# First token tiles combined with one-hot products of the last two expert tiles, in a two-layer attention and MoE step on one NeuronCore

## What is computed

```python
for l in range(2):
    x = x + gate_a * attention_l(modulate(rms_norm(x)))
    h = modulate(rms_norm(x))
    # top-1 group of 4, then top-2 experts in it, weights w0, w1
    y = w0 * expert[e0](h) + w1 * expert[e1](h)
    #   expert[e](h) = (silu(h @ w_gate[e]) * (h @ w_up[e])) @ w_down[e]
    x = x + gate_m * y
out = rms_norm(x)
```

## Time and profile before

| What | Value |
|---|---|
| Median of three runs | 1315.37 us (1311.35 to 1317.37) |
| The profiled execution, its own time | 1312.94 us |
| Its span | 1311.1 us |
| PE busy | 1223.5 us, 93% |
| DVE busy | 588.3 us, 45% |
| ACT busy | 412.6 us, 31% |
| POOL busy | 55.9 us |
| Mean DMA rate | 221 GB/s |

### The profile page before, as it was taken

How to read it: one execution, slowest core, us unless ns; L and a number is a source line. 1 busy time by engine, 2 the same in 40 slices (tenths; PEclk the granted TensorE clock), 3 DMA queues, 4 the chain that set the end, 5 groups by cost and what they waited for, 6 DMA issues and landing times.

```text
span 1311.1 us, 17016 instructions
## 1 busy us (share of the span) xinstructions
PE 1223.5 (93%) x5449; PEld 670.6 (51%) x5450; DVE 588.3 (45%) x1352; ACT 412.6 (31%) x847; POOL 55.9 (4%) x63
## 2 busy tenths in 40 slices
PE   5899999999999999998967999799999999999995
PEld 2555566666664475443323444466654574444442
DVE  0431455555543674222317443888835653222216
ACT  2333344444451120111123324677732111111113
POOL 0103000000000020000020000000000110000002
PEclk8999999999999999999987999899999999999997
DMA  9969999622253066999975000500020269989956
GB/s 374 406 261 414 414 412 411 263 98 97 98 216 130 33 251 202 353 352 355 374 303 229 9 0 21 240 1 1 1 97 1 111 227 323 345 286 322 355 225 240
DMA packets 88356, 290.17 MB, mean 221 GB/s; under 512 B 9209, under 2 KB 27580, under 8 KB 86876
## 3 DMA queue, kind: packets, MB, share of 16 engines
q1 hardware_dynamic: 46032, 185.68, 38.5%
q0 software_dynamic: 16640, 64.59, 12.5%
q10 hardware_dynamic: 25612, 38.96, 8.7%
HBM read 214.48 MB, written 74.73 MB: 221 GB/s over the span
## 4 chain that ended last, share of the span: by engine, by line
PE 82%; DMA 5%; DVE 4%; ACT 3%; SPq 2%; issue 2%; POOL 0%; ACTq 0%; DVEq 0%; POOLq 0%
PE ps L2044 16%; PE ps L1668 12%; PE ps L1685 10%; PE ps L2073 8%; PE ps L1621 7%; PE ps L1928 6%; PE ps L1891 4%; PE ps L1713 3%; PE ps L1990 3%; PE ps L1762 3%; PE ps L2125 3%; PE ps L1636 2%; SPq L479 2%; DMA arena<-in_moe_gu 2%; PE ps L1884 2%
## 5 line engine op out<-in xcount | busy, mean ns | idle before, releaser
L2044 PE MATMUL ps<-arena 128*128 (+1 forms) x560 | 246.2, 592 | 0.0
L1621 PE MATMUL ps<-const,arena 128*128 128x128 f32 (+2 forms) x1000 | 145.9, 280 | 38.6 <-DVE arena L1090 17.1
L1621 PEld LDWEIGHTS ps<-const,arena 128*128 128x128 f32 (+2 forms) x1000 | 116.8, 143 | 98.0 <-issue 43.8
L2044 PEld LDWEIGHTS ps<-arena 128*128 128x128 f32 x560 | 103.8, 190 | 117.2 <-issue 117.2
L1668 PE MATMUL ps<-arena 128*128 128x512 f32 (+2 forms) x400 | 155.7, 546 | 8.4 <-DVE arena L1101 4.8
L1139 DVE TENSOR_REDUCE hst<-ps 128x1 f32<-128x640 f32 (+1 forms) x160 | 110.9, 714 | 94.3 <-PE ps L1928 80.2
L1685 PE MATMUL ps<-arena 128*128 128x512 f32 x320 | 142.0, 596 | 1.4 <-issue 1.4
L2073 PE MATMUL ps<-arena 128*128 (+1 forms) x280 | 126.1, 593 | 2.2 <-ACT arena L836 2.2
L723 ACT ACTIVATE arena<-ps,hst 128x640 f32<-128x640 f32 (+1 forms) x160 | 112.4, 706 | 44.0 <-DVE hst L1139 44.0
L1668 PEld LDWEIGHTS ps<-arena 128*128 128x128 f32 x400 | 76.0, 194 | 81.2 <-issue 63.2
L1685 PEld LDWEIGHTS ps<-arena 128*128 128x128 f32 x320 | 59.1, 190 | 69.8 <-issue 69.7
(11 more groups left out here) (211 smaller groups left out, 1187.4 us busy)
## 6 DMA issues: line engine op xcount, KB each, us to landing
arena<-in_moe_gu SPq DMA_DIRECT2D x128, 512.0 KB, 12.6
arena<-in_ada_w SPq DMA_DIRECT2D x62, 768.0 KB, 11.7
slot_rows<-arena POOLq DMA_DIRECT2D x10, 4096.0 KB, 68.4
arena<-in_moe_w_down SPq DMA_DIRECT2D x64, 512.0 KB, 15.4
slot_rows<-arena ACTq DMA_DIRECT2D x33, 512.0 KB, 9.2
arena<-slot_rows ACTq DMA_DIRECT2D x124, 128.0 KB, 13.1
arena<-mod_rows SPq DMA_DIRECT2D x12, 512.0 KB, 10.4
arena<-in_gqa_w_qkv SPq DMA_DIRECT2D x12, 512.0 KB, 14.6
```

What stands on the lines that cost most here:

```text
L1621: return nc.tensor.transpose(out, in_, ident[0:rows, 0:rows])
L2044: last = mm(bank(gu_bank(u)), e_xsT[:, nth(u, D)][:, k * P:(k + 1) * P], w(k * BANK, BANK), start=k == 0, stop=k == KD - 1)
```

## The change

In each layer the first `EARLY[l]` token tiles (one in layer 0, two in layer 1) are combined in two parts. The expert rows that lie in the last two expert tiles (k = 2 and k = 3) aren't gathered. They are taken from `e_y` in SBUF by matmuls with one-hot matrices that hold the tokens' weights. The other rows are gathered already when the store of tile k = 1 has landed. Where a token's row lies in the last two tiles, the gather's index and its weight are made zero.

- `early_tables(l)`, on DVE behind `hid` of k = 1, computes the indices `early_i`, the weights `early_w` and the one-hot matrices `early_hot`.
- PE transposes these matrices in the tail at k = 1 (`early_turned`), DVE copies them to `early_rows`.
- POOL issues `2 * EARLY[l]` gathers once k = 1 is stored, and the rest when the last stores have landed.
- `early_sum` (DVE) weights, gates and adds the gathered part to `xt(t)`; after the last `down` PE multiplies the one-hot matrices with the two last results; `rest_sum` (DVE) gates this part and adds it.
- In layer 1 tiles 0 and 1 leave `last_sums`: their sum stands in `xt(t)`.
- `qkv1` and `qkv2` wait for the last stores, no longer for a gather. `turn_tables` (four DVE instructions, L1261 before) moves behind `mod_cols(1, 0)`.
- Some semaphores of the two layers are merged, with counts to match.

```diff
+EARLY = (1, 2)
...
             if b == 1:
-                sp.wait_ge(gathered(0, 1), gathers(0, 0))
+                sp.wait_ge(S("last_stored"), LAST_STORED)
...
-            pool.wait_ge(S("last_stored"), 16 * (RING_N + 1) * (l + 1))
-            for t in range(NTILE):
+            pool.wait_ge(S("early_tables"), 2 * l + 1)
+            pool.wait_ge(S("prior_stored"), l + 1)
+            pool.wait_ge(S("third_stored"), 16 * (l + 1))
+            for t in range(EARLY[l]):
+                for c in range(2):
+                    pool.indirect_dma_start(
+                        early_e[t][:, c * D:(c + 1) * D], None, slots,
+                        bass.IndirectOffsetOnAxis(ap=early_i[:, 2 * t + c:2 * t + c + 1], axis=0))\
+                        .then_inc(S(f"early_landed{t}"), 16)
+            pool.wait_ge(S("last_stored"), LAST_STORED * (l + 1))
+            for t in range(EARLY[l], NTILE):
...
                 hidT(R * RING_N + k, k)
+                if k == 1:
+                    dve.wait_ge(S("early_turned"), l + 1)
+                    nc.vector.tensor_copy(early_rows[:, 0:2 * EARLY[l] * P], bank(5, 2 * EARLY[l] * P)).then_inc(S("early_ready"), 1)
                 if k + 2 < SLOT_TILES - LOOPED:
                     xsT(R * RING_N + (k + 2), k + 2, R)
                 if k + 1 < SLOT_TILES - LOOPED:
                     hid(R * RING_N + (k + 1), k + 1)
+                if k == 0:
+                    early_tables(l)
...
+            op(nc.vector.tensor_tensor(split(sel, 2), bmid(index, 2), blast(last, TT), ALU.is_equal))
+            op(nc.vector.tensor_tensor(split(sel, 2), split(sel, 2), bmid(s_row, 2), ALU.mult))
+            op(nc.vector.tensor_reduce(rows, split(sel, 2), AX.X, ALU.add))
+            op(nc.vector.tensor_tensor(split(d, 2), bmid(slot, 2), blast(rows, e), ALU.subtract))
...
+            for t in range(n):
+                for i in range(2):
+                    out = hot(early_hot, t, i)
+                    a, b = e * i + 2 * t, e * i + 2 * t + 1
+                    nc.vector.tensor_scalar(out, iota, d[:, a:a + 1], w[:, 2 * t:2 * t + 1], ALU.is_equal, ALU.mult)
+                    op(nc.vector.tensor_scalar(second, iota, d[:, b:b + 1], w[:, 2 * t + 1:2 * t + 2], ALU.is_equal, ALU.mult))
+                    last_hot = op(nc.vector.tensor_tensor(out, out, second, ALU.add))
...
+        def early_sum(l, t):
...
+            nc.vector.tensor_scalar(a, a, early_w[:, 2 * t:2 * t + 1], None, ALU.mult)
+            settle()
+            nc.vector.scalar_tensor_tensor(a, b, early_w[:, 2 * t + 1:2 * t + 2], a, ALU.mult, ALU.add)
+            settle()
+            nc.vector.tensor_tensor(a, a, gate_m[:, v * D:(v + 1) * D], ALU.mult)
+            settle()
+            nc.vector.tensor_tensor(xt(t), xt(t), a, ALU.add)
...
+        def rest_sum(l, t):
...
+                nc.vector.tensor_tensor(rest, rest, gate_m[:, v * D:(v + 1) * D][:, c], ALU.mult)
+                settle()
+                last = nc.vector.tensor_tensor(xt(t)[:, c], xt(t)[:, c], rest, ALU.add)
...
         experts(0)
-        turn_tables()
-        combine(0, 0)
+        early_sum(0, 0)
+        rest_sum(0, 0)
         row_stats("mix1", 0, 1)
+        dve.wait_ge(S("last_stored"), LAST_STORED)
         norm(1, 0)
         mod_cols(1, 0)
+        turn_tables()
         combine(0, 1)
...
-        combine(1, 0)
-        combine(1, 1)
-        for t in range(NTILE):
-            if t + 2 < NTILE:
-                combine(1, t + 2)
-            final(t)
+        for t in range(EARLY[1]):
+            early_sum(1, t)
+        for t in range(EARLY[1]):
+            rest_sum(1, t)
+        final(0)
+        final(1)
+        combine(1, 2)
+        combine(1, 3)
+        final(2)
+        combine(1, 4)
+        final(3)
+        final(4)
...
                 turn_hid(R * RING_N + k, u)
+                if k == 1:
+                    pe.wait_ge(S("early_tables"), 2 * l + 2)
+                    for j in range(2 * EARLY[l]):
+                        last = turn(bank(5, P, j * P), early_hot[:, j * P:(j + 1) * P])
+                    last.then_inc(S("early_turned"), 1)
                 if more:
                     plan_of = gate_up(R * RING_N + (k + 1), u + 1, w, R * RING_N + k)
                 planned_down(R * RING_N + k, u, plan_of, not more)
+
+            pe.wait_ge(S("early_ready"), l + 1)
+            last_t = R * RING_N + (SLOT_TILES - LOOPED - 1)
+            for t in range(EARLY[l]):
+                for n in range(2):
+                    c = slice(n * BANK, (n + 1) * BANK)
+                    mm(bank(sum_bank(t) + n), hot(early_rows, t, 0), last_y[0][:, c], start=True, stop=False)
+                    if t == 0:
+                        pe.wait_ge(S("y_out", l), last_t + (2 + n))
+                    mm(bank(sum_bank(t) + n), hot(early_rows, t, 1), last_y[1][:, c], start=False, stop=True)\
+                        .then_inc(S("rest_made"), 1)
```

More of the change, by code:

```diff
@@ L295, in program, with hot, later @@
     w_pair = e_r[:, R_W:R_W + 2 * NTILE]
-    def gathered(t, c):
-        return S("gathered_first" if t == c == 0 else f"gathered{t}")
+    early_e = (e_xs[:, D:3 * D], e_xsT[:, D:3 * D])
+    early_hot, early_rows, early_tmp = ar(10752, 4 * P), ar(11264, 4 * P), ar(8448, 256)
+    early_w = early_tmp[:, 0:4]
+    last_y = (e_y[:, 2 * D:3 * D], e_y[:, 0:D])
+    LAST_STORED = 16 * 3
+    def hot(rows, t, i):
+        return rows[:, (2 * t + i) * P:(2 * t + i + 1) * P]
+    def later(l, t):
+        return sum(NTILE - n for n in EARLY[0:l]) + t - EARLY[l] + 1
     def gathers(l, t):
-        return (32 if t else 16) * (l + 1)
+        return 32 * sum(t >= n for n in EARLY[0:l + 1])
     def sum_bank(t):
@@ L1564, in experts, with early_tables, new @@
                     hid(R * RING_N + (k + 1), k + 1)
-        def combine(l, t):
+                if k == 0:
+                    early_tables(l)
+        def early_tables(l):
+            n, TT = EARLY[l], SLOT_TILES
+            e = 2 * n
+            stage = ar(14848 + 2 * TT * NE, 4 * TT + NE + 1)
+            s_row, s_rounds = stage[:, 0:TT], stage[:, 4 * TT + NE:]
+            at = [4]
+            def new(cols):
+                at[0] += cols
+                return early_tmp[:, at[0] - cols:at[0]]
+            w, last, rows, sel = new(e), new(2), new(2), new(2 * TT)
+            d, inside, keep, second = new(2 * e), new(2 * e), new(e), new(P)
+            slot = rt(R_PL, e)
+            index, iota = const[:, C_TT:C_TT + TT], const[:, C_IO:C_IO + P]
+            for i in range(2):
+                nc.vector.tensor_scalar(last[:, i:i + 1], s_rounds, float(RING_N), float(SLOT_TILES - LOOPED - 2 + i), ALU.mult, ALU.add)
+            for c in range(2):
+                nc.vector.tensor_copy(split(w, n)[:, :, c], w_pair[:, c * NTILE:c * NTILE + n])
+            settle()
[3 more added lines that the diff above has]
+            op(nc.vector.tensor_tensor(split(d, 2), bmid(slot, 2), blast(rows, e), ALU.subtract))
+            op(nc.vector.tensor_scalar(inside, d, 0.0, None, ALU.is_ge))
+            op(nc.vector.scalar_tensor_tensor(inside, d, float(P), inside, ALU.is_lt, ALU.mult))
+            op(nc.vector.tensor_tensor(keep, inside[:, 0:e], inside[:, e:2 * e], ALU.add))
+            op(nc.vector.tensor_scalar(keep, keep, -1.0, 1.0, ALU.mult, ALU.add))
+            nc.vector.tensor_tensor(early_w[:, 0:e], w, keep, ALU.mult)
+            op(nc.vector.tensor_tensor(keep, slot, keep, ALU.mult))
+            op(nc.vector.tensor_copy(early_i[:, 0:e], keep)).then_inc(S("early_tables"), 1)
+            for t in range(n):
+                for i in range(2):
+                    out = hot(early_hot, t, i)
[3 more added lines that the diff above has]
+                    last_hot = op(nc.vector.tensor_tensor(out, out, second, ALU.add))
+            last_hot.then_inc(S("early_tables"), 1)
+            settle()
@@ L1573, in combine @@
+        def combine(l, t):
+            dve.wait_ge(S("scaled"), later(l, t))
             a, b = e_g[t][:, 0:D], e_g[t][:, D:2 * D]
```

112 lines of the change are left out of this document (64 added, 48 removed).

## The result

| What | Before | After |
|---|---|---|
| Median of the runs | 1315.82 us (1311.35 to 1317.37) | 1330.67 us (1330.28 to 1336.27) |
| Profiled execution, its own time | 1312.94 us | 1336.27 us |
| Its span | 1311.1 us | 1334.5 us |

The ratio (of the means) is 1.0132 [1.0107, 1.0156], so +17.3 us. One run of 1840 us, in which the granted clock averaged 0.66 and not 0.97, is left out. The medians are of four runs before and three after. The forecast of 1312.3 us, its range and its sign were wrong: the changed kernel is slower by over 0.5%, to which I had given 0.09.

The account below looks back on a forecast made before the run. PE carries 82% of the span, so steps count where PE waits. Layer 0's -5.0 and layer 1's +1.9 sum to -3.1 us: 1309.8 against the profiled 1312.94, 1312.3 against the median 1315.37; range 1304.5 to 1319.5.

Parts of the forecast that it names:

- slower by over 0.5%: Whole kernel: needs tables at over 0.4 us per instruction or a sum of two bad rivals; chance 0.09.
- DVE is free at 1269.6 and from there bounds the end: End of layer 1, in old times: DVE starts two `early_sum` (9.6 us) at 1269.6; last scaling starts at 1304.4.
- if DVE waits for early rows in layer 1: Layer 1's end: one of the signs named in advance that would show the prediction wrong; no size given.
- the tables, 2.2 and 4.3 us: MoE tails: PE stalls 2.0 and 3.8 us before `gate_up(2)`, transposes add 0.2 and 0.4, in layers 0 and 1.
- clock lost in layer 1's stall: Rival, layer 1's tail: work restarts at the low clock, +1.8 us, 1314.1 us, with layer 0 too 1315.9; chance 0.10.
- Handover of layer 0: Between the layers: the norm starts at 688.0 instead of 693.00, 5.0 us earlier with the tables' 2.2 us paid.
- the early rows come late: Rival, layer 0's handover: gathers slowed by full DMA engines, gain gone, 1316 to 1317.5 us; chance 0.13.
- The fallen clock in the first projection products: After PE's 6.4 us idle in the handover: clock taken as fallen, transposes and first products as slow as before.
- The end of layer 1: Last scaling 2.4 us earlier without the tables; with their 4.3 us, layer 1 is 1.9 us later.
- the DVE instruction counts: `early_tables` and one-hot groups on DVE: 21 and 27 instructions in 4.7 and 6.5 us, layers 0 and 1.
- PE's one-hot products hidden in layer 0: Layer 0's handover: four products (3.5 us) end at 682.4, before `early_sum` ends at 683.3.
- no wait for `qkv1` or `qkv2`: Layer 1's projection: gathers and weight pieces end at about 703, while `qkv2` is wanted at 709.3.

Follow-up runs that it names:

- the first experiment: The changed kernel with only DVE's wait for the final norm's row moved behind the two `rest_sum` of layer 1; 1.0063 against the kernel before.
- both: The changed kernel with the norm-row wait behind `rest_sum` and the one-hot transposes and their copy at k = 2; 0.9979 against the kernel before.
- the tables alone: The kernel before with `early_tables`, one-hot transposes at k = 1 and DVE's copy added, results unused, some semaphores merged; 1.0086 against the kernel before.
- the new order: Moved norm-row wait and transposes, plus layer 1's `combine` of tile 2 before the first `final`, tiles 3 and 4 before the second; 0.9943 against the kernel before.

## Why the prediction was wrong

In ratios: +1.32% = +0.84% (PE waits for the tables) + 0.69% (DVE waits for the norm row) - 0.21% (the rest). The miss is 20.4 us, from -3.1 forecast to +17.3 measured. The norm row is 9.1 of it, the tables 4.8 (11.3 for 6.5), and the two gains, smaller than forecast, are the other 6.5.

- **The step that failed: "DVE is free at 1269.6 and from there bounds the end".** DVE was idle, but not free: its next instruction in the program was a wait for the final norm's row. The row lands after the last stores, and `before` paid nothing for that, because the gathers that followed came later still. The change moved work up behind an unmoved wait. It cost 9.1 us, the largest single part of the miss. I named this wait in no rival. Had I listed what stands ahead of `early_sum` on DVE, the issue on ACT behind the last store and the landing time would have given it. Nor was DVE free without that wait. I had named it as a sign of being wrong if DVE waits for early rows in layer 1, and it does so in every kernel in which the norm row's wait is moved, 0.84 us in the first experiment and 2.37 in "both":

```profile
1270.07 0.75 DVE L1647 TENSOR_SCALAR arena<-arena 128x1024 f32<-128x1024 f32 x1 [2.37 <-DMA arena<-slot_rows,early_i]
```

- **A term mis-sized: the tables, 2.2 and 4.3 us.** They cost 2.8 and 5.4 us up to `gate_up(2)` (the experiment with the tables alone), and 1.7 and 1.4 us more by the clock: 11.3 against 6.5. The count of 21 and 27 instructions was right, and so were the 15 small ones (3.0 us). A one-hot `tensor_scalar`, with two operations on 128x128, took 0.34 to 0.35 us where I took 0.26: a group of three takes 1.05 us (one L1634 to the next, 656.49 to 657.54), not 0.87. That makes 0.4 and 0.7 us; in layer 1 the transposes at the low clock add most of the rest (1.12 us for four in the change). The trace of `before` had nearer rows than those I put 0.26 between. The first has one operation, the second two and reads from PSUM:

```profile
L1148 DVE TENSOR_SCALAR arena<-arena,hinv 128x128 f32<-128x128 f32 x32 | 9.2, 286 | 2.5
...
L1101 DVE TENSOR_SCALAR arena<-ps,modc 128x128 f32<-128x128 f32 x80 | 26.4, 403 | 28.1 <-PE ps L1621 28.0
```

- **The rival "clock lost in layer 1's stall", 0.10, was part of what happened.** I left the clock up because the stalls stayed under 5.0 us; that argued from one fall in a longer idle stretch as if it were a threshold. It is none: in the same handover the clock fell 5.2 us after PE's last product in "both" and 2.6 us after it (684.78) in the kernel with the sums on PE first, whose window with the fall is this:

```profile
687.00:688.00 1.00, 0.00 (x0) 0.00 (x0) 1.00 (x1) 0.00 (x0) 0.69 (x2) 0.68 0.86 246
```

The Trainium skill, "TensorE: Matmul & The Clock Gate", section "HAM oscillation — how this bites in real kernels", has waits of a few microseconds between bursts throttle PE again. The traces agree: after stalls of 4.4 us the clock was down in all three profiles, after those of 2.4 us in two of three.
- **Handover of layer 0: -3.9 where I had -7.2 without the tables.** The steps from `early_sum` on held: 9.5 us to the norm (687.86 to 697.38), forecast 9.5. What was short is ahead of it: from the store's issue to POOL 8.8 us for 7.2, and from there to the second row 8.3 us for 6.7. These are 3.3 us, the difference. This is the rival "the early rows come late", of its size in part. The fallen clock in the first projection products was forecast; it cost 1.2 us more than before. That cost too varies: in "both", as in the first experiment, the clock was back when the projection began; in the other changed kernels the same 32 records took 16.3 to 17.1 us.

```profile
695.78 14.00 PE L1774 MATMUL ps<-arena 128*128 128x512 f32 x32 [1.88 <-DVE arena L1128]
```

- **The end of layer 1: -2.4 without the tables.** Even without the norm wait it was +0.8 (37.3 against 36.5 us). Of these 3.2 us, 2.4 are early rows that came late. Counted from the start of the last `down`, the first `early_sum` was forecast 0.6 us ahead of it (1269.6 against 1270.25) and began 1.7 us behind it (1270.07 against 1268.33), since the store of k = 1 took 4.9 us and not 3.0. From there to the end of `combine(4)` the steps held to 0.4 us. The last sum was then 1.1 us slower than forecast (2.92 us on PE for 1.8). DVE's two waits for ACT (2.41 and 2.31 us) stood in the forecast's sum as well, taken as given; the new order has no such waits and took 4.7 us less.
- **Right:** the DVE instruction counts, `early_sum` and `rest_sum` (7.6 us, forecast 7.7), PE's one-hot products hidden in layer 0, no wait for `qkv1` or `qkv2`.

What stays open: why the stretch ahead of the first tail differs by up to 5.7 us between executions, and whether a part of that belongs to the change; +1.0 us between the projection and layer 1's tail; why the early rows take over 8 us; and whether the stall of 2.4 us loses the clock in most runs (two of three profiles show it).

## What to carry to other kernels

When work is moved earlier, list every wait that stands ahead of its new place on its engine, those included that cost nothing now: such a wait was hidden by what the move takes away. New small work for a busy engine belongs where its inputs are already done; one pipeline step later was worth 0.8% here, since a stall of a few microseconds can be paid twice, as idling and by the clock (1.0 to 1.7 us more here). Where an idle engine feeds a chain, issue what feeds it ahead of work that only has to be done by the end.

## What the runs showed of the hardware

- With stalls of 2.4 and 4.4 us inside dense work the granted clock fell to its lower level, in layer 0 about 1 us after PE had begun again, and the 16 records behind took 8.74, 8.57, 8.42 or 8.05 us instead of 7.03. A stall of the same 2.41 us left it up in another execution.
- In the handover between the layers the clock fell 2.6 us after PE's last product in one kernel's profile and 5.2 us after it in another's, with the same instructions there.
- A one-hot `tensor_scalar` with two operations on fp32 128x128 takes 0.34 to 0.35 us. With one operation it is 0.286 us on 128x128 (L1148 before) and 0.353 on 128x256.
- A 512 KB store took 8.0 us where the DMA share was 1.03 and 4.7 us in the same place of layer 1, where the engines had been idle before it. From POOL's first early gather to the arrival of tile 0's second row it took 8.3 to 8.7 us, with and without a weight load beside them.
